# The expert value stage of a GLA, retention and PEER block: gathered sums over 1024 columns held in PSUM, lower weights formed on GpSimd, value loads in halves

## The reference

```
q = (xt @ w_q); scores = q . subkeys; two top-16 lists, top 16 of their 256 sums    # 8 heads
experts, gates = 8 heads x 16 = 128 experts a token out of 128 x 128 = 16384
act = gelu(einsum('tkd,td->tk', u_tab[experts], xb))
out = einsum('tk,tkd->td', gates * act, v_tab[experts])
h   = layer_norm(alpha * h + out)
```

## Time and profile before

| | |
|---|---|
| median of 3 runs | 1941.58 us (1937.61 to 1943.91) |
| the profiled execution's own time | 1941.25 us |
| its span, first to last instruction | 1939.4 us |
| TensorE busy | 1909.3 us, 98% |
| VectorE busy | 1348.5 us, 70% |
| GpSimd busy | 1402.8 us, 72% |
| mean granted clock of TensorE | 0.996 |

### The profile page before, as it was taken

One profiled execution on the slowest core, in us unless ns is written; L12 is line 12 of the kernel. 1 busy time (PEld: TensorE's weight loads), 2 busy tenths in 40 slices (PEclk: granted clock), 3 DMA queues, 4 the chain that ended last, 5 costly groups with the idle time before them and its releaser, 6 DMA issues.

```text
span 1939.4 us, 34300 instructions
## 1 busy us (share of the span) xinstructions
PE 1909.3 (98%) x10830; PEld 1666.6 (86%) x10830; DVE 1348.5 (70%) x2305; ACT 986.0 (51%) x1518; POOL 1402.8 (72%) x962
## 2 busy tenths in 40 slices
PE   9999999999999999999999999999999999999996
PEld 8999888888998888888888888888888888788885
DVE  1844012214688877755899999997888888788887
ACT  5544434436445556567455454545555554455553
POOL 6877878887879889888788777876465565466531
PEclk9999999999999999999999999999999999999998
DMA  8555657577869787777877777777899999999983
GB/s 301 173 152 164 206 152 226 177 234 178 211 150 207 184 188 183 168 186 189 247 168 177 173 172 172 173 172 243 288 336 330 333 327 346 384 328 329 327 315 122
DMA packets 179352, 440.59 MB, mean 227 GB/s; under 512 B 27392, under 2 KB 38528, under 8 KB 162000
## 3 DMA queue, kind: packets, MB, share of 16 engines
q1 hardware_dynamic: 163856, 384.52, 68.7%
q0 software_dynamic: 14416, 50.61, 7.6%
q10 hardware_dynamic: 1008, 4.52, 0.7%
HBM read 426.79 MB, written 12.78 MB: 227 GB/s over the span
## 4 chain that ended last, share of the span: by engine, by line
PE 79%; POOL 6%; issue 5%; DMA 5%; DVE 3%; ACT 1%; DVEq 1%; SPq 0%; POOLq 0%; ACTq 0%
PE ps L1809 23%; PE ps L1764 21%; PE ps L1765 10%; PE ps L1504 7%; PE ps L1506 7%; PE ps L1505 7%; POOL w_lo L1390 4%; DMA v_raw<-in_peer_v 4%; PE ps L1746 3%; POOL u_lo L1428 2%; DVE v_lo L1283 1%; DMA u_raw<-in_peer_u 1%; PE ps L1620 1%; ACT v_hi L734 0%; DMA raw<-in_w_in 0%
## 5 line engine op out<-in xcount | busy, mean ns | idle before, releaser
L1428 POOL TENSOR_TENSOR u_lo<-u_t,u_hi 128x512 fp32r<-128x512 f32 x512 | 653.7, 1301 | 130.4 <-ACT u_hi L641 127.3
L1764 PE MATMUL ps<-xT,u_hi 128*128 128x512 f32 x2048 | 727.1, 399 | 0.4 <-POOL u_lo L1428 0.4
L1765 PE MATMUL ps<-xT,u_lo 128*128 128x256 f32 x2048 | 573.1, 280 | 0.0
L1390 POOL TENSOR_TENSOR w_lo<-raw,w_hi 128x1024 fp32r<-128x1024 f32 x174 | 431.2, 2490 | 99.2 <-ACT w_hi L510 92.8
L641 ACT ACTIVATE u_hi<-u_t 128x512 fp32r<-128x512 f32 x512 | 321.1, 632 | 352.6 <-DVE u_t L1056 351.9
L1764 PEld LDWEIGHTS ps<-xT,u_hi 128*128 128x128 f32 x2048 | 384.6, 188 | 90.4 <-issue 0.7
L1056 DVE STREAM_TRANSPOSE u_t<-u_raw 128x512 f32<-128x512 f32 x512 | 355.1, 701 | 100.7 <-PE ps L1765 59.3
L1765 PEld LDWEIGHTS ps<-xT,u_lo 128*128 128x128 f32 x2048 | 386.6, 189 | 0.0
L510 ACT ACTIVATE w_hi<-raw 128x1024 fp32r<-128x1024 f32 x175 | 184.9, 1059 | 273.7 <-PE ps L1506 264.8
L1453 POOL DMA_INDIRECT sp_rows<-in_peer_v,sp_at x128 | 155.9, 1218 | 195.0 <-DVE far_sum L1267 170.6
L1809 PE MATMUL ps<-v_hi,m_hi 128*128 128x512 f32 x868 | 267.9, 378 | 7.9 <-DVE m_lo L1279 7.1
(11 more groups left out here) (233 smaller groups left out, 2690.7 us busy)
## 6 DMA issues: line engine op xcount, KB each, us to landing
u_raw<-in_peer_u SPq DMA_DIRECT2D x512, 256.0 KB, 4.8
v_raw<-in_peer_v SPq DMA_DIRECT2D x126, 1024.0 KB
raw<-in_w_in SPq DMA_DIRECT2D x111, 512.0 KB, 3.8
raw<-in_w_out SPq DMA_DIRECT2D x32, 512.0 KB, 4.0
raw<-in_w_peer_q SPq DMA_DIRECT2D x128, 128.0 KB, 4.4
act_dram<-act_w ACTq DMA_DIRECT2D x4, 1024.0 KB, 6.8
act_dram<-far_act SPq DMA_DIRECT2D x64, 64.0 KB, 5.1
x_again<-in_x SPq DMA_DIRECT2D x1, 2048.0 KB, 8.0
```

What stands on the lines that cost most here:

```text
L1390: pool.tensor_tensor(w_lo[:, k, :], raw[:, k, :], w_hi[:, k % HI_RING, :].bitcast(F32), ALU.subtract).then_inc(lo_done, 1)
L1428: pool.tensor_tensor(u_lo[:, r, :], u_t[:, r, :], u_hi[:, r, :].bitcast(F32), ALU.subtract).then_inc(ulo_done, 1)
L1764: pe.matmul(acc, u_hi[:, r, c], xT[:, :, kt, :], start=kt == 0, stop=False)
L1765: ins = pe.matmul(acc[:, 0:T], u_lo[:, r, c], xT_hi[:, kt, :], start=False, stop=kt == KT - 1)
```

## The change

- `FAR` goes from 768 to 1024. `far_sum` moves from SBUF to banks 6 and 7 of PSUM, and the five row buffers hold 1024 columns. TensorE no longer computes anything of columns 1024 to 2047 for the second token half: 18 products of 512 columns a tile.
- `row_add` reads and writes PSUM. In place of a drain before each addition it waits for the count of the addition before it; a drain is left before the first addition of a group.
- `m_lo` of tiles 4 to 123 is made by GpSimd (`m_low`), in the same queue as the gathers. `row_gather(k)` and `act_gather` are issued behind `m_low(i)`, where the addition that frees their buffer belongs to a tile before i. TensorE waits for a count of its own (`mlo_done`) at the start of each tile. `v_lo_done` is counted up right behind `v_lo` of the first half.
- A tile's values are loaded by two DMAs of 0.5 MB, each issued when its half of the slot is free, with 4 KB a partition in place of 8 KB. ScalarE still waits for both.
- The ten transfers of `beside` are issued one in four tiles, in iterations 17 to 26, the last value tiles first.
- At the end, the bank of columns 1024 to 1535 of the second token half no longer comes from TensorE; its statistics are made first, and the order of two PSUM copies changes.

```
-FAR = 768
+FAR = 1024
+        sp_rows = [at(f"sp_rows{s}", HT + (16 + 4 * s) * K if s < 4 else WRK + 32 * K, [P, FAR]) for s in range(S_SLOTS)]
+        far_sum = bank(6, 2)
...
+            def load_v(i, s, freed=None):
+                for h in range(2):
+                    if freed is not None:
+                        sp.wait_ge(v_free, freed + 2 * s + h + 1)
+                    sp.dma_start(v_raw[:, 2 * s + h, :], v_rows[bass.ds(i, 1), :, half_row(h)].rearrange("i j d -> j (i d)")).then_inc(v_in[s], 16)
...
+            for ii in range(P // 8 + 1, P // 8 + 11):
+                for s in range(4):
+                    load_v(ii * 4 + s, s, ii * 8)
+                beside(ii - P // 8 - 1)
...
             def row_add(n, j):
                 c, k = j % S_SLOTS, n * S_PAIR + j
-                dve.drain()
+                if j in (0, S_CHUNK[0]):
+                    dve.drain()
+                dve.wait_ge(row_added, k + 1)
...
             def v_low(ii, s, half, added=()):
                 dve.wait_ge(v_hi_done, ii * 8 + 2 * s + 1)
-                dve.tensor_tensor(v_lo[:, 2 * s, :], v_raw[:, 2 * s, :], v_hi[:, 2 * (s % 2), :].bitcast(F32), ALU.subtract)
+                ins = dve.tensor_tensor(v_lo[:, 2 * s, :], v_raw[:, 2 * s, :], v_hi[:, 2 * (s % 2), :].bitcast(F32), ALU.subtract)
+                if isinstance(ii, int) and ii == 0:
+                    dve.wait_ge(m_hi_done, s + 1)
+                    m_low(m_lo[:, s % 2, :], m_hi[:, s % 2, :], s, 0, v_lo_done)
+                else:
+                    ins.then_inc(v_lo_done, 1)
                 for n, j in added:
                     row_add(n, j)
-                dve.wait_ge(m_hi_done, ii * 4 + s + 1)
-                m_low(m_lo[:, s % 2, :], m_hi[:, s % 2, :], ii * 4 + s, half, v_lo_done)
...
             for k in range(S_PAIR):
                 act_gather(k)
-            for k in range(S_SLOTS, P):
-                row_gather(k)
-                if k - S_SLOTS + S_PAIR < P:
-                    act_gather(k - S_SLOTS + S_PAIR)
+            def add_tile(k):
+                n, j = divmod(k, S_PAIR)
+                h = j // S_CHUNK[0]
+                return 4 * (S_FIRST + 2 * n + h) + (j - h * S_CHUNK[0]) * 4 // S_CHUNK[h]
+            def m_low(i):
+                pool.wait_ge(m_hi_done, i + 1)
+                pool.tensor_tensor(by_four(m_lo[:, i % 2, :]), tile_w(i // (P // 2), i % (P // 2)), by_four(m_hi[:, i % 2, :].bitcast(F32)), ALU.subtract).then_inc(mlo_done, 1)
+            k = S_SLOTS
+            for i in range(4, P - 4):
+                m_low(i)
+                while k < P and add_tile(k - S_SLOTS) < i:
+                    row_gather(k)
+                    if k - S_SLOTS + S_PAIR < P:
+                        act_gather(k - S_SLOTS + S_PAIR)
+                    k += 1
...
             def v_tile(i, s):
-                for h in range(2):
-                    pe.wait_ge(v_lo_done, 2 * i + h + 1)
-                    for a in range(TT):
-                        ins = v_products(s, h, a)
-                    ins.then_inc(v_free, 1)
+                if not isinstance(i, int):
+                    pe.wait_ge(mlo_done, i - 3)
+                pe.wait_ge(v_lo_done, 2 * i + 1)
+                v_products(s, 0, 0)
+                v_products(s, 0, 1).then_inc(v_free, 1)
+                pe.wait_ge(v_lo_done, 2 * i + 2)
+                v_products(s, 1, 0).then_inc(v_free, 1)
```

More of the change, by code:

```diff
@@ L780, in _ @@
                 last_scaled(0, b, 1)
-            for b in range(3):
-                act.wait_ge(bank_read, 5 + b)
+            for b in (2, 0, 1):
+                if b < 2:
+                    act.wait_ge(bank_read, 5 + b)
                 act.activation(bank(4 + b), ln2b_sb[:, b * COL:(b + 1) * COL], ACT.Copy).then_inc(shift_ps, 1)
@@ L1301, in _ @@
                 v_low(0, s, 0)
-            dve.memset(far_sum[:], 0.0)
+            dve.memset(far_sum, 0.0).then_inc(row_added, 1)
             dve.wait_ge(gate_in, 16)
@@ L1323, in _ @@
                     far = h1_again[:, 1, D - FAR:]
-                    dve.scalar_tensor_tensor(far, far, float(ALPHA), far_sum[:], ALU.mult, ALU.add).then_inc(far_added, 1)
+                    dve.scalar_tensor_tensor(far, far, float(ALPHA), far_sum, ALU.mult, ALU.add).then_inc(far_added, 1)
                 if s % 2 == 0:
@@ L1341, in last_bank @@
                 c = slice(b * COL, (b + 1) * COL)
-                if (a, b) != (1, 3):
+                if a == 0 or b < 2:
                     dve.wait_ge(sum_done, 4 * a + b + 1)
-                    n = HALF - FAR if (a, b) == (1, 2) else COL
-                    o = h1_again[:, a, b * COL:b * COL + n]
-                    dve.scalar_tensor_tensor(o, o, float(ALPHA), bank(4 * a + b)[:, 0:n], ALU.mult, ALU.add).then_inc(bank_read, 1)
+                    dve.scalar_tensor_tensor(h1_again[:, a, c], h1_again[:, a, c], float(ALPHA), bank(4 * a + b), ALU.mult, ALU.add).then_inc(bank_read, 1)
                 dve.drain()
@@ L1806, in v_products @@
                 for p, (m, v) in enumerate(((mh, vh), (mh, vl), (ml, vh))):
-                    for c in cs if (a, h) != (1, 1) else (0,):
-                        n = COL if (a, h) != (1, 1) else HALF - FAR
-                        ins = pe.matmul(bank(4 * a + 2 * h + c)[:, 0:n], m, v[:, c * COL:c * COL + n], start=start and p == 0, stop=stop and p == 2)
+                    for c in cs:
+                        ins = pe.matmul(bank(4 * a + 2 * h + c), m, v[:, c * COL:(c + 1) * COL], start=start and p == 0, stop=stop and p == 2)
                 return ins
@@ L1839, in _ @@
             for a in range(TT):
-                for b in range(4 - a):
+                for b in range(4 - 2 * a):
                     for s in (2, 3, 0, 1):
```

65 lines of the change are left out of this document (25 added, 40 removed).

## The result

The changed kernel takes 1964.16 us in the median (1956.35 to 1966.85, four runs) beside 1942.22 for the kernel before: 1.0122 times the time, interval 1.01 to 1.0143. It is 1.2% slower, where I forecast 1923 and gave slower a chance of 0.24. The profiled execution took 1964.43, its span is 1962.6.

The account below looks back on a forecast made before the run. TensorE was taken to bound the kernel at 4.485 us a tile; later start, slow clock and tiles at 4.11, 4.22 and 4.37 end the stage at 1889.2, 17.4 us less, giving 1924, stated as 1923, range 1902 to 1957.

Parts of the forecast that it names:

- the part on GpSimd: v stage, GpSimd's queue: nine gather pairs and eight `m_lo` in 8 tiles take 33.7 us, 4.21 a tile.
- the sum: Tile 4's entry, slow clock and 122 tiles at 4.11, 4.22 or 4.37 end at 1889.2 us, 17.4 less than before.
- the half clock behind a stand: TensorE after its gap before tile 4: granted clock 0.50 for a while, 1.6 us, added once.
- The pair's excess: GpSimd, v stage: disturbance by `v_lo` lengthens a gather pair; its mean excess falls from 0.47 to 0.3 us.
- The second one: Rival, v stage: GpSimd and VectorE hold each other up, 4.55 to 4.75 us a tile, 1956 to 1980; chance 0.20 over 4.42.
- the break-even of 4.42: TensorE's pace in us a tile, from tile 9 on, at which the stage ends at 1906.6 as before.
- The third, the transfers: Rival, v stage: the DMA engines bound it, 4.31 us a tile at 380 GB/s, 4.65 beside side transfers, 1942; chance 0.18.
- The first, TensorE alone: Rival, v stage: TensorE stays the bound at 4.11 us a tile, 4.37 beside side transfers, 1909 to 1915; chance 0.24.
- Products, VectorE, DMA: Steps for the v stage, a tile: products 4.11 us, VectorE 3.9 to 4.2 with additions at 1.22, DMA 4.05 or 4.37.
- The DMA step: v stage transfers: 1.638 MB a tile at 405 GB/s, 4.05 us, 4.37 beside the side transfers.
- Start and end: TensorE enters tile 4 7.8 us later, waiting for `m_lo`; the end counts 0, or 1.5 if GpSimd's `ln2b` gap goes.

Follow-up runs that it names:

- e9: Changed kernel with at most three gathers between two `m_lo` in GpSimd's queue, same instructions: 1945.68 us, 1.005 times the kernel before.
- e2: Changed kernel with row gathers fetching only 512 of the 1024 columns, additions still over 1024: 1945.41 us, 1.0019 times the kernel before.
- e1: Changed kernel with `m_lo` of tiles 4 to 123 back on VectorE, behind the row additions: 1922.34 us, 0.9912 times the kernel before.
- e8: Changed kernel with `v_lo` of each tile's second half made for 8 columns only, TensorE multiplying `v_hi` instead: 1950.98 us, 1.0075 times the kernel before.
- e4: Changed kernel without the 128 activation gathers, `m_lo` still on GpSimd: 1900.22 us, 0.9794 times the kernel before.
- e5: Changed kernel with `m_lo` back on VectorE, ahead of the row additions: 1905.35 us, 0.9835 times the kernel before.
- e12: As e5, but ScalarE waits for each half's load by a count of its own: 1901.89 us, 0.9828 times the kernel before.
- e6: As e1, but a tile's values come by one load of 1 MB, 8 KB a partition: 1932.77 us, 0.9977 times the kernel before.
- e3: Kernel before with only the move of `m_lo` to GpSimd; `FAR` 768 in SBUF, loads of 1 MB: 2007.11 us, 1.0347 times the kernel before.

## Why the prediction was wrong, step by step

**The step that failed.** It is in the part on GpSimd and in the sum: "9 x 2.8 + 8 x (0.71 + 0.10 + 0.25) = 33.7 us, 4.21 a tile", taken as the pace of 77 tiles. As a sum of GpSimd's work it is nearly right: 34.1 us. In it two errors cancel. The pair takes 3.07, not 2.8 (2.61 of gathers and 0.45 of gaps, where I had 2.2 and 0.6), and `m_lo` with its gap and its disturbance 0.85, not 1.06. What failed is the use of a mean as the pace. The sum has no term for GpSimd's own waits, 3.1 us in 8 tiles (33.1 x 8 / 86), nor for what TensorE loses in the stands. I had written of "two pairs in a row ahead of it once in 8 tiles" and put no price on it. There are two buffers of `m_lo`, and `m_hi` of tile i is made when TensorE is through with tile i - 2. So GpSimd can't work ahead, and a spare microsecond in a tile with one pair doesn't pay for a tile with two. There TensorE stands up to 2.5 us, its clock falls to half behind about every second stand, it frees the buffers later, and now GpSimd and ScalarE wait for it (96.4 us of ScalarE's waits end with TensorE, 42 before). 122 x (4.60 - 4.28) = 39 us, with 1.8 more at the start, lead from 1923 to 1964. I had priced the half clock behind a stand once for the whole stage, 1.6 us; it comes seven times from 1400 to 1800 us alone. e9 shows the order's part, 0.11 to 0.17 of the 0.32 us a tile. For the rest there are GpSimd's own work (4.27 for the 4.21 of the sum), the stands that e9 leaves, and the transfers (e2 gets 0.12 from 18% fewer bytes). How these share it is open, as they were not taken apart.

**The pair's excess.** By the gathers alone, a pair is 1.90 us undisturbed and was 2.37 before. I let the excess fall from 0.47 to 0.3, since VectorE's work with two SBUF inputs falls. It rose to 0.71 (1.304 + 1.309 - 1.90), and to 0.89 in e1. The share of VectorE's time isn't what counts, but how often a gather begins within a `v_lo`: in the kernel before 64 of 196 gathers waited for one, in the changed kernel 120 of 192. A row gather is often released by the end of an addition, and soon behind that in VectorE's queue is a `v_lo`. In e1 an addition released the row gather below, which began 0.03 us after the begin of a `v_lo`:

```profile
1499.02 1.22 DVE L1291 TENSOR_TENSOR v_lo<-v_raw,v_hi 128x1024 fp32r<-128x1024 f32 x1
1499.05 2.01 POOL L1453 DMA_INDIRECT sp_rows<-in_peer_v,sp_at  x1 [0.88 <-DVE ps L1269]
```

e8 shows the same from the other side. The Trainium skill (SBUF — State Buffer, section Who interferes with whom) says that the interface that VectorE and GpSimd share is an exclusive lock, and, of VectorE's modes with two ports, that whoever issues first has it for the whole instruction. The gathers agree with it in that each waits for the end of the `v_lo` in which it began (120 of 120). They don't keep out the next one in turn: the 1.90 us gather ran its last 0.83 us beside a second `v_lo`, which took 1.22 as always.

**The rivals.** The second one came true: GpSimd and VectorE hold each other up, with a pace of 4.60 over the break-even of 4.42. But its reason was only half named. I priced it by longer `m_lo` (0.4 us of waiting for 4.55); `m_lo` was short, and the gathers and the order did it. The chance of 0.20 was too low for a case in which I had "four resources within 5% of each other". The third, the transfers, is not the cause, though e2 shows a part of theirs: with a DMA share of 0.98 ScalarE waited less for loads (74 us against 111), and e4 and e5 moved 399 to 402 GB/s. The first, TensorE alone, isn't what happened here, but it describes e4, e5 and e12 (4.16 to 4.19).

**Products, VectorE, DMA.** 18 products of 0.228 are right. The addition took 1.284 us, not 1.22. It took this in every kernel, with GpSimd busy or not, so the PSUM operand does leave the interface free. The DMA step is nearly right: I took 405 GB/s and 4 KB packets without a price, and e4, e5 and e12 moved 399 to 402 with such packets. This is the transfer row of e5 from 1450 to 1550 us:

```profile
DMA packets 11719, 39.47 MB, mean 395 GB/s; under 512 B 2088, under 2 KB 2088, under 8 KB 11719
```

The Trainium skill's 358 GB/s for one core (DMA: Bandwidth & Descriptors, section Specifications) is under what this row shows; the measurement decides. Halved loads, which I counted at nothing, gain 0.10 (by the ratios) to 0.15 us a tile (by the traces), shown by e6.

**Start and end.** Tile 4 was to enter at 1367.3, after a gap of some 10 us released by `m_lo`; it entered at 1369.12 after 10.33, with a slow clock behind it. The end was to give 0 and gave 0.1: GpSimd's `ln2b` addition stands at 1952.01 behind 4.17 us without a cause, as before:

```profile
1952.01 1.26 POOL L1498 TENSOR_TENSOR h_again<-h_again,ln2b_sb 128x512 f32<-128x512 f32 x1 [4.17 <-issue]
```

**What the change holds.** The wider gathered sums and the halved loads, with `m_lo` on VectorE ahead of the additions, make the kernel 1.7% faster (e5, e12); without the halved loads, and with `m_lo` behind the additions, it is 0.2% (e6). `m_lo` on GpSimd turns the gain into a loss of 1.2%. VectorE, 86% busy in the quiet stretch, could keep its 0.42 us a tile (it is 95% busy in e5); GpSimd, 59% busy, had no room at the right moment.

## What to carry to other kernels

An engine's mean work a tile is its pace only if it can work ahead. Before something that the bounding engine awaits in each tile goes into another queue, count the longest run of other work that can stand ahead of it there, and compare that with one tile, not with the mean. If it must go there, spread the rest, as e9 did; that gave back a good half of the loss and no gain. Gaps between instructions, which the busy share leaves out, belong to an engine's load: of GpSimd's 4.27 us a tile 0.5 are such gaps.

## What the runs showed of the hardware

- An indirect gather on GpSimd takes 0.94 to 0.96 us undisturbed, with a gap of 0.30 between two of them. With half of the columns a row gather took 1.297 us on the mean against 1.304 (e2), so its time on GpSimd doesn't go by the bytes.
- Begun just behind the begin of a `v_lo` of 1.22 us the same gather took 2.01 us (e1, at 1499.05). In the changed kernel, from 1400 to 1800 us, all 120 gathers that began within a `v_lo` ended 0.81 to 0.85 us after its end, and the next `v_lo` could run beside them.
- `m_lo` of 256 columns on GpSimd takes 0.74 to 0.75 us undisturbed, 1.47 at the longest in the stretch from 1400 to 1800 us. VectorE does it in 0.42.
- An addition of 1024 columns that reads and writes PSUM took 1.283 to 1.285 us on the mean in all kernels that had it; one that reads two SBUF tiles grew from 1.022 to 1.331 beside GpSimd's `m_lo` (e3).
- After a stand of 2.55 us TensorE's granted clock was 0.50, and ten products took 3.88 us in place of 2.28 (changed kernel, 1689.70 to 1693.58).
- The DMA engines moved 399 to 402 GB/s over 400 us (e4, e5, e12), with 4 KB a partition in the loads and the rows, and the activations' small packets among them.
